# Sums of squares of x as four 32-row tiles, a bank copy and one product, in a two-group transformer trunk on one core

## The chip, the cores and the metric

The kernel runs on one core of a Trainium2 chip. The metric is device time in microseconds (us) of one execution; lower is better. TensorE (PE in the rows) multiplies, VectorE (DVE) and ScalarE (ACT) do elementwise work, GpSimd (POOL) splits weights, and SyncE (SP) issues the weight transfers.

## What is computed

Two layers are applied to 128 context tokens and 256 latent tokens at once (384 token columns, width 1024). Each layer has three sub-layers: a SwiGLU FFN, a token mixer (differential attention, a gated recurrence, grouped attention), and a second FFN. Each is wrapped in the same way:

```python
def rmsnorm(x, g):
    xf = x.astype(jnp.float32)
    xf = xf * lax.rsqrt(jnp.mean(xf * xf, axis=-1, keepdims=True) + EPS)
    return (xf * g.astype(jnp.float32)).astype(x.dtype)

def modulate(x, g, shift, scale):
    return rmsnorm(x, g) * (1 + scale) + shift

mod = jax.nn.silu(cond) @ p['ada_w'][l] + p['ada_b'][l]
m = jnp.split(mod[:, None, :], 9, axis=-1)
h = modulate(x, p['norm_pre'][l, 0], m[0], m[1])
y = swiglu(h, p['ffn_gate'][l, 0], p['ffn_up'][l, 0], p['ffn_down'][l, 0])
x = x + 0.5 * m[2] * rmsnorm(y, p['norm_post'][l, 0])
```

So ahead of each sub-layer there is one mean of squares of x per token (the subject here), behind it one mean of squares of y, and the nine modulation vectors of a layer come from a matrix `ada_w` of 1024 x 9216.

## The kernel before

Activations lie transposed: the 1024 channels are eight tiles of 128 partitions (`KT` is 8), the 384 tokens (`T`) are the free dimension. Weights come in units of 512 KB. For a weight unit ScalarE makes a rounded copy `w_hi` (`highs`), GpSimd the rest `w_lo` (`lows`), and TensorE takes three products for each block (line 573). A modulation unit (`ada_unit`, line 612) is 128 rows of `ada_w` by 1024 columns; TensorE multiplies it by the small `c_col` in four column tiles of 32, side by side, into a bank of `MOD`.

All orders are written out by hand, one program for each engine, and semaphores tie them. The order of the transfers on SyncE's queue is the list `ALL`. A transfer into one of the four `raw` places waits until the unit that held the place has been used (`lo_ready` for weights, `ada_used` for modulation units). Eighteen further modulation units are loaded early into places named `hold`, `hold_a` and so on.

Between two sub-layers lies a gap (`gap`), of which there are five. In it TensorE first sums the squares of y (`y_sums`), runs the first half of the gap's modulation units, sums the squares of x (`x_sums`), runs the second half of the units, and goes on with the next sub-layer's weights (`by_tiles`), which wait for the normalized rows `h` tile by tile. Four of the gaps have 24 units, so 12 and 12; the last one, ahead of the second FFN of layer 1, has 8, all of them in hold places. In the four long gaps units 14 to 17, 22 and 23 use the `raw` ring; unit 22 takes the place of unit 14 and unit 23 that of unit 15. Units 14 and 15 stand behind `x_sums`.

In a gap VectorE makes 1/root of y (line 1487), updates x (1490, 1492, 1495), scales x (1454), makes 1/root of x (1465) and normalizes (1459); ScalarE squares x (1072), takes the square roots (1050) and makes `h_hi` (1079), and VectorE `h_lo` (1445).

At the start (the prologue) the same sums run with modulation units 4, 5 and 6 of a first group of 16 between them: a unit behind every second product. Those 16 units wait for their transfers only. There `first_pre` on VectorE takes the root, multiplies x by it (1425), takes the first modulation group (1322, 1324), makes the scale factors mA in three small steps (1408 to 1410), multiplies by them (1432) and takes the second group.

Of the kernel before, what the change touches and what calls it, by code (L numbers as in the profile page):

```python
# [9 lines left out]
D, SEQ, LAT, DEPTH, PAST = 1024, 128, 256, 2, 128  # L10
T = SEQ + LAT
NB = T // 128
KT = D // 128
# [43 lines left out]
def build(nc, io, out):  # L57
    f32, f32r, u8 = mybir.dt.float32, mybir.dt.float32r, mybir.dt.uint8
    ALU, ACT, AX = mybir.AluOpType, mybir.ActivationFunctionType, mybir.AxisListType
# [6 lines left out]
    def at(name, shape, dt, offset):  # L66
        size = (int(np.prod(shape[1:])) * (1 if dt == u8 else 4) + 31) // 32 * 32
        return nc.alloc_sbuf_tensor_at(name, shape, dt, offset=offset), offset + size

    x, o = at("x", [128, KT, T], f32, base)  # L70

    hold, _ = at("hold", [128, 6, 1024], f32, o)
    h_hi, o = at("h_hi", [128, KT, T], f32r, o)
    h_lo, o = at("h_lo", [128, KT, T], f32r, o)
    raw, o = at("raw", [128, RAW, 1024], f32, o)
    w_hi, o = at("w_hi", [128, SPLIT, 1024], f32r, o)
    w_lo, o = at("w_lo", [128, SPLIT, 1024], f32r, o)
    R = o
    act_hi, o = at("act_hi", [128, FT, T], f32r, R)
    act_lo, R_END = at("act_lo", [128, FT, T], f32r, o)  # L80
    x_out, _ = at("x_out", [128, NB, D], f32, R)
# [9 lines left out]
    hold_b, _ = at("hold_b", [128, 3, 1024], f32, R + FT * T * 4)  # L91
    hold_a, _ = at("hold_a", [128, 4, 1024], f32, R + 4 * T * 4)
# [19 lines left out]
    y, o = at("y", [128, KT, T], f32, Y)  # L112
    sq, o = at("sq", [128, KT, T], f32, o)
    hold_sq, _ = at("hold_sq", [128, 3, 1024], f32, o - KT * T * 4)
    silu, o = at("silu", [128, 2, T], f32, o)
    prod, o = at("prod", [128, 2, T], f32, o)
    Y_END = Y + 36864
    assert o <= Y_END
    y_sum, o = at("y_sum", [128, T], f32, o)
    root, o = at("root", [128, T], f32, o)  # L120
    ada_t, o = at("ada_t", [128, 256], f32, o)
    assert o <= Y_END
    rows, o = at("rows", [128, 3, 128], f32, Y)
    x_rows, o = at("x_rows", [128, NB, D], f32, o)

    first_w, o = at("first_w", [128, 16, 1024], f32, R)
    lam_in, o = at("lam_in", [128, DEPTH, 4, 64], f32, o)
    lam_p, o = at("lam_p", [128, DEPTH * 2, 64], f32, o)
    mask_f, o = at("mask_f", [128, 2, len(LEVELS), 64], f32, o)
    assert o <= R_END  # L130

    ctx_k, o = at("ctx_k", [128, 512], f32, Y)
    ctx_v, o = at("ctx_v", [128, 512], f32, o)
    ctx_kT, o = at("ctx_kT", [128, HA, 128], f32, o)
    v_nat, o = at("v_nat", [128, NB, 512], f32, o)
    k_nat, o = at("k_nat", [128, 512], f32, o)
    p = []
    for b in range(2):
        t_, o = at(f"p{b}", [128, 2, T], f32, o)
        p.append(t_)  # L140
    pT, o = at("pT", [128, 2, T], f32, o)
    comb, o = at("comb", [128, T], f32, o)
    rope_t, o = at("rope_t", [128, 4, LAT], f32, o)
    rope_u, o = at("rope_u", [128, 4, LAT], f32, o)
    assert o <= Y_END
    ctx_ck, o = at("ctx_ck", [128, 128], f32, Y)
    ctx_cv, o = at("ctx_cv", [128, 128], f32, o)
    c_kT, o = at("c_kT", [128, PAST + T], f32, o)
    c_kd, o = at("c_kd", [128, KVC, PAST + T], f32, o)
    c_nat, o = at("c_nat", [128, 512], f32, o)  # L150
    c_vd, o = at("c_vd", [128, KVC, 4, 2, 64], f32, o)
    assert o <= Y + 14 * 1024
    c_sq, o = at("c_sq", [128, 5, T], f32, Y + 18432)
    c_rt, o = at("c_rt", [128, 5, T], f32, o)
# [5 lines left out]
    for b in range(2):  # L160
        t_, o = at(f"dec{b}", [128, 2 * T], f32, o)
        dec.append(t_)
    lev = []
    for b in range(2):
        t_, o = at(f"lev{b}", [128, 2 * T], f32, o)
        lev.append(t_)
    W1 = o
    scores, o = at("scores", [128, HB * T], f32, o)
    v_b, o = at("v_b", [128, NB, HB, 128], f32, o)
    b_f, o = at("b_f", [128, HB * T], f32, o)  # L170
    b_b, o = at("b_b", [128, HB * T], f32, o)
    assert o == Y_END
    k_sum, _ = at("k_sum", [128, HB * T], f32, W1)
    scan_b, _ = at("scan_b", [128, HB * T], f32, S_IN)
    q_st, o = at("q_st", [128, 2, HB, LAT], f32, W0)
    k_st, o = at("k_st", [128, HB, 256], f32, o)
    assert o == W1
    o_sq, o = at("o_sq", [128, HB, T], f32, W0)
    o_rt, o = at("o_rt", [128, HB, T], f32, o)
# [7 lines left out]
    o = Y_END  # L187
    con, o = at("con", [128, C_N], f32, o)
    masks, o = at("masks", [128, 2, len(LEVELS), 64], u8, o)
    o = (o + 31) // 32 * 32  # L190
    reset, o = at("reset", [128, T], f32, o)
    vec, o = at("vec", [128, DEPTH, V_ROWS], f32, o)
    misc, o = at("misc", [128, M_ROWS], f32, o)
    mod, o = at("mod", [128, MOD_TILES, 2], f32, o)
    tick, o = at("tick", [128, 1], f32, o)
    tick_a, o = at("tick_a", [128, 1], f32, o)
    c_col, o = at("c_col", [128, KT, 32], f32, o)
    mA, o = at("mA", [128, KT, 2], f32, o)
    mB, o = at("mB", [128, KT, 2], f32, o)
    mG, o = at("mG", [128, KT, 2], f32, o)  # L200
    eps, o = at("eps", [128, 1], f32, o)
    lam_s, o = at("lam_s", [128, DEPTH, 2], f32, o)
    neg_lam, o = at("neg_lam", [128, DEPTH], f32, o)
    lb, o = at("lb", [128, DEPTH, 2, HB], f32, o)
    omlb, o = at("omlb", [128, DEPTH, 2, HB], f32, o)
    lb_d, o = at("lb_d", [128, 2, HB], f32, o)
    sub_g, o = at("sub_g", [128, DEPTH], f32, o)
    qn_g, o = at("qn_g", [128, DEPTH], f32, o)
    one_l, o = at("one_l", [128, 8], f32, o)
    lbl, o = at("lbl", [128, 2, 2, HB], f32, o)  # L210
    nmax, o = at("nmax", [128, 2, 2], f32, o)
    esum, o = at("esum", [128, 2, 2], f32, o)
    rsum, o = at("rsum", [128, 2], f32, o)
    ends, o = at("ends", [128, 2, HB * NB], f32, o)
    dend, o = at("dend", [128, 2, HB], f32, o)
    assert o <= nc.sbuf_usable_end, (o, nc.sbuf_usable_end)

    ident, ones = con[:, C_ID:C_ID + 128], con[:, C_ONE:C_ONE + 128]
    head_ones, swap = con[:, C_HEAD:C_HEAD + 128], con[:, C_SWAP:C_SWAP + 128]

    with ExitStack() as ctx:
        def pb(name, shape):
            return ctx.enter_context(nc.psum_tensor(name, shape, f32))

        X = [pb("X0", [128, 2, 512]), pb("X1", [128, 2, 512])]
        Ab = pb("Ab", [128, 512])
        S5, S6, S7 = pb("S5", [128, 512]), pb("S6", [128, 512]), pb("S7", [128, 512])
# [5 lines left out]
        def sem(name):  # L233
            return ctx.enter_context(nc.semaphore(name))
# [7 lines left out]
        x_free = [sem("x0_free"), sem("x1_free")]  # L242
        g_free = [sem(f"g{b}_free") for b in range(4)]
        names = ("const_in table_in mask_in rows_in lam_in_s lam_ready x_in xs_in rows_turned vec_ready c_ready c_zero x_turned x_copied x_ready "
                 "x_sq_ready y_sq_ready y_added sum_ready root_ready norm_ready hh_ready h_ready silu_ready act_ready "
                 "dve_step act_step half_done gate_ready gate_free sum_made mg_hi_ready ada_used ada_copied mod_taken "
                 "proj_ready ctx_in nat_ready nat_copied nat_out swap_ready rope_done scores_ready max_ready "
                 "probs_ready comb_ready turned_ready turned_copied out_ready out_taken "
# [5 lines left out]
        S = {n: sem(n) for n in names}  # L254
# [302 lines left out]
        def _(pe):  # L557
            seen = Seen()
# [126 lines left out]
            def x_sums(units):  # L685

                for k in range(KT):
                    pe.wait_ge(S["x_sq_ready"], seen.next("x_sq_ready"))
                    mm = nc.tensor.matmul(S5[:, 0:T], ones, sq[:, k, :], start=k == 0, stop=k == KT - 1)  # L689
                    if k % 2 and k // 2 < len(units):  # L690
                        ada_unit(units[k // 2])
                mm.then_inc(S["sum_ready"], 1)

            def head_sums():

# [239 lines left out]
            for b in range(NB):  # L935
# [5 lines left out]
                for k in range(KT):  # L941
                    bank = (S7, S5)[k // 4][:, :] if b == 2 else X[b][:, k // 4, :]
                    mm = nc.tensor.transpose(bank[:, k % 4 * 128:k % 4 * 128 + 128],
                                             x_rows[:, b, k * 128:k * 128 + 128], ident)
# [23 lines left out]
            for c in range(4):  # L968
                pe.wait_ge(S["x_ready"], KT + 3 * KT * DEPTH - KT + 2 * c + 2)
                for b in range(NB):  # L970
                    for k in (2 * c, 2 * c + 1):
                        mm = nc.tensor.transpose(banks[b][k // 4][:, k % 4 * 128:k % 4 * 128 + 128],
                                                 x[:, k, b * 128:b * 128 + 128], ident)
# [5 lines left out]
        def _(act):  # L979
            seen = Seen()  # L980
            A = nc.scalar.activation
# [65 lines left out]
            def root_of_sums():  # L1047

                act.wait_ge(S["sum_ready"], seen.next("sum_ready"))
                A(root[:, :], S5[:, 0:T], ACT.Sqrt, bias=eps[:, 0:1], scale=1.0 / D).then_inc(S["root_ready"], 1)  # L1050

            def gap(units):

                root_of_sums()

                act.wait_ge(S["ada_used"], units[2].n + 1)
                x_squares(0, KT)
                root_of_sums()
                act.wait_ge(S["ada_used"], units[:9][-1].n + 1)
                h_highs(0, KT)  # L1060

# [196 lines left out]
            A(omlb[:, 1, :, :], lb_d[:, :, :], ACT.Sigmoid, scale=-1.0)  # L1258
            A(tick_a[:, :], eps[:, :], ACT.Sqrt)
            x_squares(0, KT)  # L1260
            root_of_sums()
            highs(2)
            h_highs(0, 2)
            highs(SPLIT)
# [685 lines left out]
```

## Time and profile before

| | us |
|---|---|
| median of 3 runs | 2328.82 (2327.84 to 2329.07) |
| profiled execution, its own time | 2327.03 |
| its span, first to last instruction | 2325.2 |
| PE busy | 2207.0 (95%) |
| DVE busy | 961.5 (41%) |
| ACT busy | 889.8 (38%) |
| POOL busy | 1274.0 (55%) |
| mean granted TensorE clock | 0.976 |

The rows give a start, a duration, an engine, a line and the tiles that are written and read; in brackets stands how long the engine was idle before and what it waited for. An fp32 product of one matmul in the source is two instructions in the rows (x2).

### The profile page before, as it was taken

The numbers are of one execution on the slowest core, as the hardware profiler recorded it, in microseconds if no ns is written. First come the engines' busy times: TensorE is split into PE (matmuls) and PEld (weight loads), VectorE is DVE, ScalarE is ACT, GpSimd is POOL, SyncE is SP. The second block draws the span as 40 slices with busy tenths as digits, with TensorE's granted clock in tenths as the row PEclk, the third lists the DMA queues.
The fourth block names the chain that finished last, engine by engine and source line by source line (L and its number), as shares of the span: only waits on it lengthen the run. The fifth ranks groups of instructions, "written<-read, shape, count | busy, mean of one in ns | idle before, by whom it ended". The sixth has DMA issues, their size and how long they took to land.

```text
span 2325.2 us, 32769 instructions
## 1 busy us (share of the span) xinstructions
PE 2207.0 (95%) x13545; PEld 2083.2 (90%) x13545; DVE 961.5 (41%) x1532; ACT 889.8 (38%) x1181; POOL 1274.0 (55%) x988
## 2 busy tenths in 40 slices
PE   6999999998999999999999999999798999899998
PEld 4999988987899897999979999799688989799997
DVE  5221125535778365212251221634376874622112
ACT  3222223345644444233233233324474535332331
POOL 2666554433498463666646666354346954466662
PEclk8999999999999999999999999999899999899998
DMA  7555774322222274444554445633222234344431
GB/s 272 163 162 168 247 238 141 97 83 75 73 64 74 91 279 138 127 127 163 192 189 127 127 150 195 209 118 92 68 73 64 73 96 151 98 118 126 128 117 65
DMA packets 306924, 311.42 MB, mean 134 GB/s; under 512 B 9923, under 2 KB 285655, under 8 KB 306775
## 3 DMA queue, kind: packets, MB, share of 16 engines
q1 hardware_dynamic: 299671, 303.55, 41.2%
q10 hardware_dynamic: 7104, 5.77, 0.8%
q8 instruction: 107, 1.75, 0.3%
q14 instruction: 42, 0.34, 0.0%
HBM read 305.35 MB, written 3.93 MB: 133 GB/s over the span
## 4 chain that ended last, share of the span: by engine, by line
PE 77%; DVE 11%; ACT 7%; issue 2%; DMA 2%; POOL 1%; SPq 0%; ACTq 0%; DVEq 0%
PE X L573 54%; PE S L573 8%; PE Ab L573 5%; PE X L814 2%; DMA raw<-in_ada_w 1%; PE S L689 1%; ACT w_hi L990 1%; PE X L732 1%; PE S L761 1%; ACT p L1126 1%; DVE mg_lo L1376 1%; DVE y L1490 1%; PE X L712 1%; DVE x L1492 1%; DVE root L1487 1%
## 5 line engine op out<-in xcount | busy, mean ns | idle before, releaser
L514 POOL TENSOR_TENSOR w_lo<-raw,w_hi 128x512 fp32r<-128x512 f32 (+1 forms) x872 | 1168.0, 1361 | 995.8 <-ACT w_hi L990 986.0
L990 ACT ACTIVATE w_hi<-raw 128x1024 fp32r<-128x1024 f32 (+1 forms) x436 | 453.3, 1041 | 729.7 <-PE X L573 688.1
L573 PE MATMUL X<-h_hi,w_hi 128*128 128x384 f32 x1600 | 539.9, 337 | 9.1 <-DVE h_lo L1445 9.1
L573 PE MATMUL X<-h_hi,w_lo 128*128 128x384 f32 x1600 | 537.4, 336 | 0.0
L573 PE MATMUL X<-h_lo,w_hi 128*128 128x384 f32 x1600 | 537.4, 336 | 0.0
L573 PEld LDWEIGHTS X<-h_hi,w_hi 128*128 128x128 f32 x1600 | 302.5, 189 | 18.2 <-DVE h_lo L1445 10.8
L573 PEld LDWEIGHTS X<-h_lo,w_hi 128*128 128x128 f32 x1600 | 302.6, 189 | 0.0
L573 PEld LDWEIGHTS X<-h_hi,w_lo 128*128 128x128 f32 x1600 | 302.4, 189 | 0.0
L1501 DVE TENSOR_TENSOR prod<-X,silu 128x768 f32<-128x768 f32 x44 | 42.1, 958 | 571.1 <-PE X L573 571.1
L573 PE MATMUL X<-act_hi,w_hi 128*128 128x384 f32 x704 | 236.2, 335 | 0.0
L573 PE MATMUL X<-act_hi,w_lo 128*128 128x384 f32 x704 | 235.3, 334 | 0.0
L573 PE MATMUL X<-act_lo,w_hi 128*128 128x384 f32 x704 | 235.2, 334 | 0.0
L1512 DVE TENSOR_SCALAR y<-X,mG 128x128 f32<-128x128 f32 x96 | 33.4, 412 | 339.4 <-ACT prod L1094 339.4
L573 PE MATMUL S<-h_hi,w_hi 128*128 128x384 f32 x480 | 167.9, 350 | 0.0
L573 PE MATMUL S<-h_lo,w_hi 128*128 128x384 f32 x480 | 161.8, 337 | 0.0
L573 PE MATMUL S<-h_hi,w_lo 128*128 128x384 f32 x480 | 161.5, 337 | 0.0
L573 PEld LDWEIGHTS X<-act_hi,w_hi 128*128 128x128 f32 x704 | 132.1, 188 | 3.7 <-issue 3.7
L573 PEld LDWEIGHTS X<-act_lo,w_hi 128*128 128x128 f32 x704 | 132.1, 188 | 0.0
L573 PEld LDWEIGHTS X<-act_hi,w_lo 128*128 128x128 f32 x704 | 132.1, 188 | 0.0
L573 PE MATMUL Ab<-h_hi,w_hi 128*128 128x384 f32 x320 | 111.8, 349 | 0.7 <-DVE acc_e L1363 0.7
L573 PE MATMUL Ab<-h_hi,w_lo 128*128 128x384 f32 x320 | 107.9, 337 | 0.0
L573 PE MATMUL Ab<-h_lo,w_hi 128*128 128x384 f32 x320 | 107.9, 337 | 0.0
(339 smaller groups left out, 3242.8 us busy)
## 6 DMA issues: line engine op xcount, KB each, us to landing
raw<-in_w_in SPq DMA_DIRECT2D x124, 512.0 KB, 3.8
raw<-in_ffn_gate SPq DMA_DIRECT2D x88, 512.0 KB, 3.8
raw<-in_ffn_up SPq DMA_DIRECT2D x88, 512.0 KB, 3.7
raw<-in_ffn_down SPq DMA_DIRECT2D x80, 512.0 KB, 3.4
raw<-in_ada_w SPq DMA_DIRECT2D x48, 512.0 KB, 4.2
hold<-in_ada_w SPq DMA_DIRECT2D x29, 512.0 KB, 4.6
first_w<-in_ada_w SPq DMA_DIRECT2D x16, 512.0 KB, 10.5
hold_a<-in_ada_w SPq DMA_DIRECT2D x16, 512.0 KB, 6.8
```

The lines of the kernel that those rows point to most:

```text
L514: ins = nc.gpsimd.tensor_tensor(slot(w_lo, u)[:, part], raw_of(u)[:, part], slot(w_hi, u)[:, part], SUB)
L573: mm = nc.tensor.matmul(dst, w[:, k, m * 128:m * 128 + 128], r_, start=start and k + j == 0, stop=stop and k == u.nk - 1 and j == 2)
L689: mm = nc.tensor.matmul(S5[:, 0:T], ones, sq[:, k, :], start=k == 0, stop=k == KT - 1)
L712: mm = nc.tensor.matmul(X[xb][:, t // 2, t % 2 * 256:t % 2 * 256 + 256], swap, proj[:, tile0 + t, SEQ:T], start=True, stop=True)
L732: mm = nc.tensor.matmul(X[n % 2][:, c, at_:at_ + k.shape[-1]], proj[64 * c:64 * c + 64, (AQ if kind == "a" else CQ) + h, b * 128:b * 128 + ...
L761: mm = nc.tensor.matmul((S5, S6)[c][:, 0:128], v, pT[:, c, j * 128:j * 128 + 128], start=j == 0, stop=j == len(kbs) - 1)
L814: mm = nc.tensor.matmul(X[n % 2][:, 0, j * 64:j * 64 + 64], g, cols, start=True, stop=True)
L990: A(slot(w_hi, u), raw_of(u), ACT.Copy).then_inc(hi_ready[u.split], 1)
L1126: e = A(p[n % 2][:, c, 0:w], X[n % 2][:, c, 0:w], ACT.Exp, bias=nmax[:, n % 2, c:c + 1], accum_out=esum[:, n % 2, c:c + 1])
L1376: V.tensor_tensor(mg[t][1][:, t % 4, :], gate_b[:, t, :], mg[t][0][:, t % 4, :], SUB).then_inc(S["mg_ready"], 1)
L1501: V.tensor_tensor(prod[:, :, :], X[1][:, :, 0:T], silu[:, :, :], MUL).then_inc(x_free[1], 1)
L1512: ins = V.tensor_scalar(y[:, 2 * i + m, t0:t1], X[u.dest][:, m, t0:t1], mG[:, 2 * i + m, g:g + 1], None, MUL)
```

## The change

The eight products of `x_sums` (one for each tile k of squares) no longer add up in one full bank. Product k uses 32 columns of ones and writes 32 rows of the bank S5, at column tile k % 4; tiles k and k + 4 add up in the same 32 rows. ScalarE copies the bank to a new tile `part`, and one fp32 product with the full matrix of ones adds the 128 rows, each part being there 32 times, which the factor 1/(32 D) takes out again. It writes X[0]. ScalarE's root waits for that. TensorE's wait for the copy and the added product stand ahead of the modulation units that follow `x_sums`.

```diff
+    part, _ = at("part", [128, T], f32, o - T * 4)
...
             def x_sums(units):
...
                 for k in range(KT):
+                    rows_ = slice(32 * (k % 4), 32 * (k % 4) + 32)
                     pe.wait_ge(S["x_sq_ready"], seen.next("x_sq_ready"))
-                    mm = nc.tensor.matmul(S5[:, 0:T], ones, sq[:, k, :], start=k == 0, stop=k == KT - 1)
+                    mm = nc.tensor.matmul(S5[rows_, 0:T], ones[:, 0:32], sq[:, k, :], start=k < 4, stop=k >= 4,
+                                          tile_position=(0, 32 * (k % 4)))
                     if k % 2 and k // 2 < len(units):
                         ada_unit(units[k // 2])
-                mm.then_inc(S["sum_ready"], 1)
+                mm.then_inc(S["part_ready"], 1)
+
+                pe.wait_ge(S["part_copied"], seen.next("part_copied"))
+                nc.tensor.matmul(X[0][:, 0, 0:T], ones, part[:, :], start=True, stop=True).then_inc(S["sum_ready"], 1)
...
+            def root_of_parts():
+
+                act.wait_ge(S["part_ready"], seen.next("part_ready"))
+                A(part[:, :], S5[:, 0:T], ACT.Copy).then_inc(S["part_copied"], 1)
+                act.wait_ge(S["sum_ready"], seen.next("sum_ready"))
+                A(root[:, :], X[0][:, 0, 0:T], ACT.Sqrt, bias=eps[:, 0:1], scale=1.0 / (32 * D)).then_inc(S["root_ready"], 1)
...
                 x_squares(0, KT)
-                root_of_sums()
+                root_of_parts()
```

`root_of_parts` takes the place of `root_of_sums` in `gap` (behind the squares of x, not behind those of y) and in the prologue.

On TensorE in a long gap, from the first 12 modulation units on (hold places) to the second 12, before the change:

```order
L612 MATMUL S<-hold_sq,c_col 32x256 x12
L612 MATMUL S<-hold,c_col 32x256 x20
L612 MATMUL Ab<-hold,c_col 32x256 x4
L612 MATMUL Ab<-hold_c,c_col 32x256 x8
L612 MATMUL Ab<-hold_b,c_col 32x256 x4
L689 MATMUL S<-sq,con 128x384 x8
L612 MATMUL Ab<-hold_b,c_col 32x256 x8
L612 MATMUL Ab<-raw,c_col 32x256 x8
L612 MATMUL S<-raw,c_col 32x256 x8
L612 MATMUL S<-hold_a,c_col 32x256 x16
```

The same place in the changed kernel (`con` holds the ones):

```order
L614 MATMUL S<-hold,c_col 32x256 x20
L614 MATMUL Ab<-hold,c_col 32x256 x4
L614 MATMUL Ab<-hold_c,c_col 32x256 x8
L614 MATMUL Ab<-hold_b,c_col 32x256 x4
L693 MATMUL S<-sq,con 32x384 x8
L700 MATMUL X<-part,con 128x384
L614 MATMUL Ab<-hold_b,c_col 32x256 x8
L614 MATMUL Ab<-raw,c_col 32x256 x8
L614 MATMUL S<-raw,c_col 32x256 x8
L614 MATMUL S<-hold_a,c_col 32x256 x16
```

The product of line 700 now stands between the sums and unit 12; two units later come 14 and 15 (Ab<-raw), whose use lets units 22 and 23 be transferred.

On TensorE in the prologue, before the change:

```order
L612 MATMUL Ab<-first_w,c_col 32x256 x16
L689 MATMUL S<-sq,con 128x384 x2
L612 MATMUL Ab<-first_w,c_col 32x256 x4
L689 MATMUL S<-sq,con 128x384 x2
L612 MATMUL Ab<-first_w,c_col 32x256 x4
L689 MATMUL S<-sq,con 128x384 x2
L612 MATMUL Ab<-first_w,c_col 32x256 x4
L689 MATMUL S<-sq,con 128x384 x2
L612 MATMUL Ab<-first_w,c_col 32x256 x4
L612 MATMUL S<-first_w,c_col 32x256 x32
```

The same place in the changed kernel:

```order
L614 MATMUL Ab<-first_w,c_col 32x256 x16
L693 MATMUL S<-sq,con 32x384 x2
L614 MATMUL Ab<-first_w,c_col 32x256 x4
L693 MATMUL S<-sq,con 32x384 x2
L614 MATMUL Ab<-first_w,c_col 32x256 x4
L693 MATMUL S<-sq,con 32x384 x2
L614 MATMUL Ab<-first_w,c_col 32x256 x4
L693 MATMUL S<-sq,con 32x384 x2
L700 MATMUL X<-part,con 128x384
L614 MATMUL Ab<-first_w,c_col 32x256 x4
L614 MATMUL S<-first_w,c_col 32x256 x32
```

Products and units keep their order; products are 32 rows high, and line 700 stands behind the last of them.

## Rows read from the trace of the kernel before

**Rows 1.** The page, the chain that ended last, shares by engine.

```profile
PE 77%; DVE 11%; ACT 7%; issue 2%; DMA 2%; POOL 1%; SPq 0%; ACTq 0%; DVEq 0%
```

**Rows 2.** Chain through the first long gap (355 us): start, duration, what.

```profile
355.32 1.91 PE Ab L612 x32
357.23 0.02 issue
357.25 5.23 DMA raw<-in_ada_w
...
362.52 0.64 PE S L612 x8
363.16 11.99 PE X L573 x68
```

**Rows 3.** Timeline of the same gap, ScalarE, VectorE and TensorE.

```profile
353.19 0.99 ACT L1072 ACTIVATE sq<-x 128x384 f32<-128x384 f32 x2 [0.53 <-DVE x L1495]
355.36 0.58 ACT L1050 ACTIVATE root<-S,eps 128x384 f32<-128x384 f32 x1 [1.18 <-PE S L689]
360.12 0.75 DVE L1445 SCALAR_TENSOR_TENSOR h_lo<-sq,mB,h_hi 128x128 fp32r<-128x128 f32 x2
361.17 0.64 PE L612 MATMUL S<-raw,c_col 128*32 128x256 f32 x8 [1.39 <-DMA raw<-in_ada_w]
```

**Rows 4.** Timeline ahead of that gap: one lone fp32 product behind ScalarE.

```profile
340.08 0.81 ACT L1094 ACTIVATE prod<-X 128x768 f32<-128x768 f32 x1 [0.96 <-PE X L573]
340.94 0.91 PE L682 MATMUL S<-prod,con 128*128 128x384 f32 x2 [0.26 <-ACT prod L1094]
```

**Rows 5.** Groups of ScalarE by form: copies out of a bank (busy, mean ns).

```profile
L1027 ACT ACTIVATE gates<-S 128x384 f32<-128x384 f32 x22 | 10.7, 486 | 20.2 <-PE S L573 20.2
```

**Rows 6.** Waits in the second, third and fourth long gap: us in total, times, longest.

```profile
PE S L612 <- DMA raw<-in_ada_w: 2.5, 2, 1.6
...
PE S L612 <- DMA raw<-in_ada_w: 1.6, 2, 1.0
...
PE S L612 <- DMA raw<-in_ada_w: 1.3, 2, 0.7
```

**Rows 7.** Timeline of the short gap (2015 us).

```profile
2015.01 8.26 PE L689 MATMUL S<-sq,con 128*128 128x384 f32 x16 [4.13 <-ACT sq L1072]
...
2019.70 0.99 ACT L1072 ACTIVATE sq<-x 128x384 f32<-128x384 f32 x2 [0.53 <-DVE x L1495]
2023.30 0.58 ACT L1050 ACTIVATE root<-S,eps 128x384 f32<-128x384 f32 x1 [2.61 <-PE S L689]
2028.86 0.69 PE L573 MATMUL X<-h_hi,w_hi 128*128 128x384 f32 x1 [3.73 <-DVE h_lo L1445]
```

**Rows 8.** Stretches: busy by engine, then granted clock, DMA share, GB/s.

```profile
17.00:21.00 4.00, 4.00 (x25) 1.59 (x24) 0.00 (x0) 1.77 (x5) 0.00 (x0) 1.00 1.03 410
41.00:47.70 6.70, 5.69 (x18) 5.69 (x19) 4.70 (x9) 6.70 (x17) 2.47 (x2) 0.50 0.18 56
1194.70:1198.10 3.40, 3.40 (x12) 3.40 (x12) 3.40 (x12) 1.83 (x6) 0.00 (x0) 0.50 1.07 344
2014.00:2020.60 6.60, 5.59 (x9) 3.17 (x10) 6.32 (x10) 3.71 (x8) 0.00 (x0) 0.50 0.02 6
```

**Rows 9.** Timeline of the prologue.

```profile
15.36 3.41 ACT L1072 ACTIVATE sq<-x 128x384 f32<-128x384 f32 x8 [4.76 <-DVE x L1820]
15.60 0.64 PE L612 MATMUL Ab<-first_w,c_col 128*32 128x256 f32 x8 [0.17 <-DMA first_w<-in_ada_w]
...
23.93 0.58 ACT L1050 ACTIVATE root<-S,eps 128x384 f32<-128x384 f32 x1 [5.16 <-PE S L689]
30.09 5.41 POOL L514 TENSOR_TENSOR w_lo<-raw,w_hi 128x512 fp32r<-128x512 f32 x4 [29.65 <-ACT w_hi L990]
34.34 1.19 DVE L1410 TENSOR_TENSOR mA<-mA,vec 128x16 f32<-128x16 f32 x1
35.57 3.76 DVE L1432 TENSOR_SCALAR sq<-sq,mA 128x128 f32<-128x128 f32 x16
40.03 0.18 DVE L1403 TENSOR_TENSOR mB<-mod,vec 128x16 f32<-128x16 f32 x1
42.01 0.69 PE L573 MATMUL X<-h_hi,w_hi 128*128 128x384 f32 x1 [5.33 <-DVE h_lo L1445]
```

More of the change, by code:

```diff
@@ L244, in build @@
         names = ("const_in table_in mask_in rows_in lam_in_s lam_ready x_in xs_in rows_turned vec_ready c_ready c_zero x_turned x_copied x_ready "
-                 "x_sq_ready y_sq_ready y_added sum_ready root_ready norm_ready hh_ready h_ready silu_ready act_ready "
+                 "x_sq_ready y_sq_ready y_added sum_ready part_ready part_copied root_ready norm_ready hh_ready h_ready silu_ready act_ready "
                  "dve_step act_step half_done gate_ready gate_free sum_made mg_hi_ready ada_used ada_copied mod_taken "
@@ L1260, in _ @@
             x_squares(0, KT)
-            root_of_sums()
+            root_of_parts()
             highs(2)
```

## The prediction

> **What bounds the kernel now.** I read the chain that ended last first. TensorE holds 77% of it [rows 1], so work that only VectorE or ScalarE does counts where TensorE stands still for it. The sums of x stand in six places: the prologue, four long gaps and one short gap. For each the question is which wait of TensorE ends last behind the sums, so I followed the chain through each place, and then the timeline.
>
> In the first long gap the chain runs from the sums' end at 355.32 through the modulation units behind them, and at 357.25 it leaves TensorE for a transfer of a modulation unit (5.23 us), returns for the last unit at 362.52 and goes on with the weights at 363.16 [rows 2]. The transfer is that of unit 23 into the raw place of unit 15. It can't be issued before unit 15 has been used, and unit 15 stands behind the sums. So the start of the next sub-layer hangs on the *end of the sums on TensorE*, not on the root. The rows of h are early: the first h_lo is made by 360.87, 2.3 us ahead of the weights' start [rows 3]. In the other three long gaps TensorE waits for the same two transfers, 2.5, 1.6 and 1.3 us [rows 6].
>
> In the short gap all units are in hold places. There TensorE waits 3.73 us for h_lo [rows 7], so the root decides. In the prologue TensorE waits 5.33 us for h_lo too [rows 9], and the root decides through VectorE's long row of steps.
>
> **The change part by part, long gap.** Before: ScalarE's last square of x ends at 354.18 (353.19 + 0.99), and the root starts at 355.36, 1.18 us later [rows 3]. After:
>
> - The last square's product. In the full array it had to queue behind that of k = 6; in its own 32 columns it can start at once, at 354.23 (a product starts 0.05 after the ScalarE instruction that releases it: 340.89 to 340.94 [rows 4]). How long does a lone product last in a 32-column tile? A modulation unit is such a product with 256 columns, four side by side: 0.64 us for all four [rows 9]. The two passes of 384 columns take 2 x 128 columns more; a lone full product of 384 columns takes 0.91 [rows 4]. Between 0.64 and 0.91 I take 0.64 and the added columns at 2 x 0.107, less what the rows round, 0.84: end at 355.07. That is 0.25 earlier than now (355.32).
> - The copy. Out of a bank, 128x384, 0.486 us [rows 5], from 355.11 (the root starts 0.04 behind the sums' end now, 355.32 to 355.36) to 355.59.
> - The product. 0.05 and 0.91 [rows 4]: 355.64 to 356.56. The root starts at 356.60.
>
> So the root and everything that TensorE does behind the sums come 356.60 - 355.36 = **1.24 us later**. No table is loaded for the copy: ScalarE already makes copies (w_hi) between roots and squares. Nothing else is queued on ScalarE between squares and root; on TensorE the 12 units are queued behind the wait, and SyncE's queue waits for two of them, with the transfers of the next weights behind. Units 14 and 15, the two issues, the transfers, the last unit and the weights' start all move by 1.24. The rows of h move by the same and keep their 2.3 us. Behind the gap TensorE is the bound again, so nothing gives the time back. Four long gaps: **+4.96**. Bounds for one gap: +1.49 if the tiles don't run side by side (nothing saved ahead of the copy), and about 0 if the last transfers didn't depend on the sums.
>
> Where would the work that the tiles save show? Eight full products take 0.64 each in a row, 5.1 us, four tiles side by side about 1.3. The Trainium skill (TensorEngine Tiling (Array Packing), section Theoretical Speedup) gives up to four times for such tiles; by it alone a gap would lose 3.9 us. The trace disagrees for the gaps: TensorE waits for squares, which wait for x, and only the last 1.14 us (354.18 to 355.32) lie behind the last square.
>
> **Short gap.** The clock is at half (0.50, the 1.2 GHz level) from 2014.0 to 2020.6 [rows 8], after TensorE stood idle for 4.13 us. At that level the full products fall behind the squares: the last square ends at 2020.69, the root starts at 2023.30, 2.61 later [rows 7]. With tiles side by side the first six products keep up (two squares come every 1.9 us, two tiles take 1.3 to 1.5 at half clock), the last ends at about 2021.6, and copy and product bring the root to 2023.15: **-0.1**. If the clock is still at half then, both products take longer and the root comes at 2024.6: +1.3.
>
> **Prologue.** The squares are all there at 18.77 (15.36 + 3.41), TensorE finishes the sums at 23.9 [rows 9]: here TensorE is behind. A pair of products side by side takes 0.64 plus a tail, a unit 0.43; the sums are then held by unit 6, which stands ahead of the last pair. Unit 3 was waited for at 15.60 [rows 9]; at 410 GB/s [rows 8] 0.524 MB need 1.28 us, so unit 6 lands at 19.44. The last pair ends at 19.9 + 0.83 = 20.7, the copy at 21.3, the product at 22.2; the root starts at 22.26 instead of 23.93, 1.67 earlier.
>
> Not all of it arrives. GpSimd makes w_lo from 30.09 to 35.5 [rows 9], and while it does, VectorE's steps take as long as GpSimd's: 1.19 us for 128x16 at 34.34, against 0.18 for such a step at 40.03. The two take turns. Now the copy to mod and the three mA steps lie in that time, and the 16 multiplications follow alone at 35.57 in 3.76. Moved 1.67 ahead, VectorE gets through the copy and two steps before 30.09; the third step and about three multiplications then take a turn each, and the other 13 (3.76 x 13/16 = 3.0) begin at 35.1 to 35.5. They end at 38.1 to 38.5 instead of 39.3, 0.8 to 1.2 earlier; I take 1.0. TensorE starts its weights at 41.0 instead of 42.01. There the clock is at half until 47.7 [rows 8]; 1.0 us at half is worth 0.5 at full clock: **-0.5**. Bounds: 0, and -2.3, if the clock also comes back one stretch of 3.4 us (as that at 1194.7 [rows 8]) earlier, because TensorE is busy sooner (-1.7 more).
>
> **Sum.** 4 x 1.24 - 0.1 - 0.5 = +4.4. The profiled execution took 2327.03, 1.8 under the median of the runs; on its own time that gives 2331.4, on the median of 2328.82 **2333.2 us**. A measurement of this kernel tells 0.2% (4.7 us) from no change, so the forecast lies just inside that.
>
> **The rivals.**
>
> - *The clock falls more often.* TensorE uses a quarter or half of its columns in the sums and stands still for another 0.6 us per gap. One more stretch of 3.4 us at half costs up to 1.7 us where TensorE is the bound. For: the short gap and the stretch at 1194.7 [rows 8] show that such idle times cost clock; against: modulation units in 32-column tiles leave it at full in the other long gaps. Two or three stretches more: +7.8 to +9.5, 2336.6 to 2338.3.
> - *The tiles don't run side by side.* Gaps +1.49 x 4, short gap +1.3, prologue about +0.3: +7.6, 2336.4. Against it, four tiles of a unit fit in 0.64 us [rows 9].
> - *The delay is hidden in the long gaps*, because the transfers have their own reason to end late, or h's slack takes it: -0.6 to +0.6, 2328 to 2329.5. Against it is the chain of rows 2.
> - *Faster: TensorE is what is behind in the gaps.* This decides as soon as the squares wait ready for TensorE; the tiles must save more than the 1.49 of copy and product, and now 1.14 in all lie behind the last square in a long gap. With all eight squares ready a gap's sums would take 1.3 + 0.2 + 1.49 = 3.0 instead of 5.3, -2.3 in five gaps, with the prologue -12, 2317. The skill's page on tiling would have it so. For it speaks only the short gap at half clock.
>
> **How the numbers follow.** As forecast, one stretch of clock more or less included (+2.7 to +6.1, 2331.5 to 2335): 0.58, of it 0.31 under +4.7 and 0.27 over. Clock 0.15, tiles in series 0.06, hidden 0.16, faster by the tiles or by several stretches of clock 0.05. Faster by over 0.2%: 0.05; within: 0.31 + 0.16 = 0.47; slower: 0.27 + 0.15 + 0.06 = 0.48. The range runs from 2329.0 (the upper part of hidden, or -2.3 in the prologue with a stretch less) to 2338.0 (two stretches more).
>
> **What would show it.** Root of x 2.4 us behind the last square instead of 1.18 in the long gaps; units 22 and 23 issued and the weights started 1.24 later, seen from the root of y; in the short gap the root 2.5 behind the last square; in the prologue the root near 22.3, but TensorE's first weights only near 41. Wrong would be: weights that start no later in the long gaps (the transfers were not tied to unit 15), sums' products that follow each other at 0.64 in a tile column, or a granted clock with other half stretches than now.

## The result, and the profile after

| | before | after |
|---|---|---|
| median of 12 runs each | 2328.45 us | 2333.57 us |
| lowest to highest | 2324.96 to 2331.08 | 2330.14 to 2336.73 |
| ratio, 95% interval | 1 | 1.0023 (1.0016 to 1.0031) |
| span of the profiled execution | 2325.2 us | 2333.7 us |
| granted clock over the span | 0.976 | 0.975 |

The changed kernel is 5.1 us slower by the medians, just over the 0.2% (4.7 us) that can be told from no change. The two profiled spans differ by more, 8.5 us. All tables below say which of the two they use.

**Where TensorE is held.** The page of the kernel after, the chain that ended last, shares by engine. It answers to [rows 1] and has hardly moved; a change of 5 us in 2330 can't be seen there.

```profile
PE 77%; DVE 11%; ACT 7%; issue 2%; DMA 1%; POOL 1%; SPq 0%; ACTq 0%; DVEq 0%
```

**The first long gap.** First ScalarE's timeline of the kernel after, which answers to the ScalarE rows of [rows 3]: start, duration, operation, and in brackets the idle time ahead and what ended it.

```profile
351.81 0.99 ACT L1087 ACTIVATE sq<-x 128x384 f32<-128x384 f32 x2 [0.52 <-DVE x L1510]
353.73 0.49 ACT L1063 ACTIVATE part<-S 128x384 f32<-128x384 f32 x1 [0.92 <-PE S L693]
355.22 0.58 ACT L1065 ACTIVATE root<-X,eps 128x384 f32<-128x384 f32 x1 [1.00 <-PE X L700]
```

The last square ends at 352.80 and the root starts at 355.22, 2.42 us later; before it was 1.18 [rows 3]. Between them now stand two waits of ScalarE, 0.92 and 1.00, with the copy in the middle. TensorE's timeline of the same gap:

```profile
352.39 1.30 PE L693 MATMUL S<-sq,con 128*32 128x384 f32 x4 [0.21 <-ACT sq L1087]
354.27 0.91 PE L700 MATMUL X<-part,con 128*128 128x384 f32 x2 [0.58 <-ACT part L1063]
355.12 1.07 PE L614 MATMUL Ab<-hold_b,c_col 128*32 128x256 f32 x16
...
360.83 0.64 PE L614 MATMUL S<-raw,c_col 128*32 128x256 f32 x8 [1.19 <-DMA raw<-in_ada_w]
362.12 0.64 PE L614 MATMUL S<-raw,c_col 128*32 128x256 f32 x8 [0.65 <-DMA raw<-in_ada_w]
362.69 0.45 PE L575 MATMUL X<-h_hi,w_hi 128*128 128x384 f32 x1
```

The sums end at 353.69, 0.89 behind the last square (before 1.14): that is all that the tiles give here. Then TensorE waits 0.58 for the copy, and the product takes 0.91. Only at 355.12 do the twelve modulation units begin. The chain through the gap, as in [rows 2]:

```profile
353.73 0.50 ACT part L1063
354.23 0.04 issue
354.27 0.91 PE X L700 x2
355.19 1.91 PE Ab L614 x32
357.10 0.02 issue
357.11 4.96 DMA raw<-in_ada_w
...
362.12 0.64 PE S L614 x8
362.76 12.36 PE X L575 x70
```

It is the chain of [rows 2] with two links put in front, the copy and the product: then four units, the transfer of unit 23, the last unit, the weights. One row of VectorE's timeline, which answers to the h_lo row of [rows 3], shows that the rows of h still don't decide; they are there at 360.73, 2.0 us ahead of the weights:

```profile
359.98 0.75 DVE L1460 SCALAR_TENSOR_TENSOR h_lo<-sq,mB,h_hi 128x128 fp32r<-128x128 f32 x2
```

TensorE's waits for transfers in the second, third and fourth long gap (us in total, times, longest) answer to [rows 6]:

```profile
PE S L614 <- DMA raw<-in_ada_w: 3.4, 2, 1.9
...
PE S L614 <- DMA raw<-in_ada_w: 1.8, 2, 1.0
...
PE S L614 <- DMA raw<-in_ada_w: 1.2, 2, 0.6
```

In the third and fourth the waits are about as long as before (1.6 and 1.3): everything, issue and landing, has moved by the same amount. In the second they are 0.9 longer.

**The short gap.** Timelines of TensorE and ScalarE of the kernel after, as in [rows 7]:

```profile
2023.31 6.76 PE L693 MATMUL S<-sq,con 128*32 128x384 f32 x16 [4.13 <-ACT sq L1087]
2030.65 0.91 PE L700 MATMUL X<-part,con 128*128 128x384 f32 x2 [0.58 <-ACT part L1063]
2028.01 0.99 ACT L1087 ACTIVATE sq<-x 128x384 f32<-128x384 f32 x2 [0.53 <-DVE x L1510]
2031.61 0.58 ACT L1065 ACTIVATE root<-X,eps 128x384 f32<-128x384 f32 x1 [1.00 <-PE X L700]
```

The root starts 2.61 behind the last square (2029.00 to 2031.61), as before. The sums take 6.76 instead of 8.26, and copy and product take it all back. Over the traces it varies a little: 2.42 to 2.63 in the five that have tiles there, 2.60 to 2.83 in the four with full sums and no added steps.

**The prologue.** Timelines of TensorE, ScalarE, VectorE and GpSimd, as in [rows 9]. The multiplications (L1447) stand three times: all of them, those that begin before 35.0, and those from there on, each from a view of its own:

```profile
16.67 0.86 PE L693 MATMUL S<-sq,con 128*32 128x384 f32 x4
20.18 0.82 PE L693 MATMUL S<-sq,con 128*32 128x384 f32 x4
21.59 0.91 PE L700 MATMUL X<-part,con 128*128 128x384 f32 x2 [0.59 <-ACT part L1063]
22.54 0.58 ACT L1065 ACTIVATE root<-X,eps 128x384 f32<-128x384 f32 x1 [1.00 <-PE X L700]
30.20 0.17 DVE L1424 TENSOR_SCALAR mA<-mA 128x16 f32<-128x16 f32 x1
30.29 4.99 POOL L516 TENSOR_TENSOR w_lo<-raw,w_hi 128x512 fp32r<-128x512 f32 x4 [29.84 <-ACT w_hi L998]
30.41 1.17 DVE L1425 TENSOR_TENSOR mA<-mA,vec 128x16 f32<-128x16 f32 x1
31.61 6.76 DVE L1447 TENSOR_SCALAR sq<-sq,mA 128x128 f32<-128x128 f32 x16
31.61 3.74 DVE L1447 TENSOR_SCALAR sq<-sq,mA 128x128 f32<-128x128 f32 x3
35.28 3.09 DVE L1447 TENSOR_SCALAR sq<-sq,mA 128x256 f32<-128x256 f32 x13
41.05 0.69 PE L575 MATMUL X<-h_hi,w_hi 128*128 128x384 f32 x1 [4.13 <-DVE h_lo L1460]
```

The root starts at 22.54 instead of 23.93, the weights at 41.05 instead of 42.01. GpSimd's four steps end at 35.28. Of the 16 multiplications three stand beside them and take 3.67 us from start to start (1.22 each, as long as a step of GpSimd); the other 13 follow in 3.09 (0.24 each).

**Each stage.** Both traces, us. "Root to root" is from the start of the root of y to that of x. The prologue's row has the two absolute times.

| | root to root, before | after | root of y to weights, before | after | moved |
|---|---|---|---|---|---|
| prologue (times of root and weights) | 23.93 | 22.54 | 42.01 | 41.05 | -0.96 |
| long gap 1 | 12.82 | 14.06 | 20.55 | 21.53 | +0.98 |
| long gap 2 | 12.82 | 14.06 | 20.95 | 23.52 | +2.57 |
| long gap 3 | 12.82 | 14.06 | 20.07 | 21.49 | +1.42 |
| long gap 4 | 13.17 | 14.41 | 20.13 | 21.28 | +1.15 |
| short gap | 14.25 | 14.25 | 19.81 | 19.81 | 0.00 |

The last column sums to +5.2; I call it the *stage sum*. The rest of the 8.5 us between the spans, 3.4 us, lies between the stages, from the weights' start to the next root of y, where the clock stands otherwise. Windows of the kernel after: the stretch, busy by engine, then granted clock, DMA share, GB/s.

```profile
40.00:46.30 6.30, 5.25 (x16) 5.25 (x17) 4.26 (x9) 6.30 (x16) 2.02 (x2) 0.50 0.37 119
899.60:906.50 6.90, 6.21 (x24) 5.40 (x25) 6.62 (x20) 4.66 (x11) 0.00 (x0) 0.51 0.73 251
```

The first is the stretch at half that [rows 8] has at 41.0 to 47.7: it now ends at 46.3. The second is not in the trace before. It begins in the second long gap, behind 1.50 and 1.89 us in which TensorE waited for the last two transfers. The change is not needed for it: the kernel of the first experiment, whose gaps are those of before, is at half from 898.2 to 901.6, behind waits of 1.63 and 1.86. Leaving out the stretches at the very end of the program, the trace before has 95.6 us at half and that after 105.8; with them it is 112.0 and 118.5.

### The profile page after: what moved, and what is told of

Read it like the earlier page. It is cut to its first block, busy times and chain, and to the rows that moved or that the text cites. A ratio compares the mean times of both kernels' runs of the same rounds, so it can differ in the third digit from the quotient of the medians.

```text
span 2333.7 us, 32799 instructions
## 1 busy us (share of the span) xinstructions
PE 2207.2 (95%) x13557; PEld 2077.8 (89%) x13557; DVE 960.2 (41%) x1532; ACT 892.7 (38%) x1187; POOL 1273.0 (55%) x988
## 4 chain that ended last, share of the span: by engine, by line
PE 77%; DVE 11%; ACT 7%; issue 2%; DMA 1%; POOL 1%; SPq 0%; ACTq 0%; DVEq 0%
PE X L575 54%; PE S L575 8%; PE Ab L575 4%; PE X L822 2%; DMA raw<-in_ada_w 1%; ACT w_hi L998 1%; PE X L740 1%; DVE y L1505 1%; PE S L769 1%; ACT p L1141 1%; PE Ab L614 1%; DVE mg_lo L1391 1%; DVE root L1502 1%; DVE x L1507 1%; PE X L720 1%
```

## The experiments

All are kernels of their own, with the kernel before run beside them on the same chip. Three changes of code are used in them: the *sums* (full array or tiles), the *split* of a long gap's units (12 ahead of the sums and 12 behind, or 16 and 8), and what stands between sums and root (nothing, or copy and product).

### The prologue alone

The tiles, copy and product stay in the prologue; the gaps have the full sums of the kernel before again (`x_sums_full`).

```diff
                 for u in units[:len(units) // 2]:
                     ada_unit(u)
-                x_sums([])
+                x_sums_full([])
...
                 x_squares(0, KT)
-                root_of_parts()
+                root_of_sums()
```

> Tiled sums with copy and product in the prologue only; the five gaps sum as before. Theory (each long gap pays the copy and the product, the prologue gains): the root of the prologue near 22.4 instead of 23.93, the weights start near 41.0, every gap 12.8 us from the root of y to the root of x as before, and the time 0.5 to 1.4 us under before: 2327.0 to 2328.0. Rival (the clock, not the gaps, made the changed kernel slower): the time lies between before and the changed kernel by chance, with no difference in the gaps. Rival (GpSimd's turns swallow the prologue's gain): weights start at 42.0, time as before.

Measured: 2327.46 against 2327.32, ratio 0.9998 (0.9989 to 1.0006). Root at 22.53, weights at 40.94, the gaps' roots where they are before (12.82 in the first three, 1.18 behind the last square). The prologue gives about a microsecond at the weights' start, and the time of the whole kernel, of which I had expected 0.5 to 1.4 less, can't tell that from nothing.

### The gaps alone

```diff
-            x_sums(PHASES["first"][4:7])
+            x_sums_full(PHASES["first"][4:7])
...
             x_squares(0, KT)
-            root_of_parts()
+            root_of_sums()
```

> Tiled sums in the five gaps only; the prologue sums as before. Theory: from the root of y to the root of x 14.06 us in the long gaps (1.24 more than 12.82), about 14.2 in the short one, and the time 4 x 1.24 = 5.0 us over before and about 1 over the changed kernel: 2333.5 to 2334.5. Rival (the clock made the difference): nearer to before than +2.5.

Measured: 2336.2, ratio 1.0037 (1.0024 to 1.005). All four long gaps have the root 2.42 behind the last square and root to root 14.05 (14.40 in the fourth), +1.23 or +1.24 each. The loss is in the gaps. It is larger than expected by about 2 us: 3.1 us more were lost to the clock in its executions than in those of the kernel before (below), and its prologue was late by 0.9 (weights at 42.92).

### Full sums, but copy and product kept

It tells the price of the two added steps from the gain of the tiles. (The sum over all 128 partitions is taken twice here, so the scale is 1/(128 D).)

```diff
-                    mm = nc.tensor.matmul(S5[rows_, 0:T], ones[:, 0:32], sq[:, k, :], start=k < 4, stop=k >= 4,
-                                          tile_position=(0, 32 * (k % 4)))
+                    mm = nc.tensor.matmul(S5[:, 0:T], ones, sq[:, k, :], start=k == 0, stop=k == KT - 1)
```

> The sums are full products in the whole bank as before, but the copy and the added product stay (scale 1/(128 D)), in all six places. Theory: the tiles save 0.25 in a long gap, so without them a long gap takes 12.82 + 1.49 = 14.3 us from root to root, the short gap 1.5 to 1.8 more than with tiles or before (15.8), and the prologue's root comes at 25.4 instead of 22.5; in all 4 x 1.49 + 1.5 + 0.2 to 0.5 = +7.7 to +8.0 over before: 2336.3. Rival (the tiles save nothing, or cost, because TensorE changes its tile mode): long gaps at 14.06 as in the changed kernel or under it.

Measured: 2337.79, ratio 1.0041 (1.0026 to 1.0056), 10.5 over before where I had expected 7.7 to 8.0. The weights start 9.9 later in sum: 6.5 in the long gaps, 1.7 in the short one and 1.7 in the prologue, for which I had put 0.2 to 0.5. TensorE's timeline of its first long gap:

```profile
353.16 3.02 PE L693 MATMUL S<-sq,con 128*128 128x384 f32 x8 [0.37 <-ACT sq L1086]
356.76 0.91 PE L699 MATMUL X<-part,con 128*128 128x384 f32 x2 [0.58 <-ACT part L1062]
```

The root comes 2.67 behind the last square: copy and product with their latencies cost 2.67 - 1.18 = 1.49 in a long gap, and the tiles save 2.67 - 2.42 = 0.25 of it. In the short gap, where TensorE is behind at half clock, the tiles save 4.29 - 2.61 = 1.68, and the steps cost the same (before, without either, it is 2.61 too); in the prologue the tiles save 25.53 - 22.54 = 3.0, and the steps cost about 1.2 (25.53 less 24.37, the mean of the root in the three traces that have full sums and no added steps there: 23.93, 24.79 and 24.38).

### All eight products in one tile column

As after, but the products use rows 0 to 31 of the bank, one behind the other, as one sum of eight (`start=k == 0, stop=k == KT - 1`); the copy has 32 rows and the product contracts over 32.

```diff
-                    rows_ = slice(32 * (k % 4), 32 * (k % 4) + 32)
+                    rows_ = slice(0, 32)
...
-                                          tile_position=(0, 32 * (k % 4)))
+                                          tile_position=(0, 0))
```

> The changed kernel with all eight products in the same 32 columns and rows, one behind the other; the copy takes 32 rows, the product 32 rows of part. Theory (what the tiles save is that products of different column tiles run side by side): in a long gap the last product waits for the one before, so the root of x comes 0.25 later than in the changed kernel, 14.3 us behind the root of y, and in the prologue each pair takes 1.3 us instead of 0.8, so that the root comes near 24.5 to 25.4 instead of 22.5. Rival (it is the 32 columns that are faster, not the four places): both as in the changed kernel.

Measured with a single execution: 2338.71, against 2328.68; the root comes 2.57 behind the last square in the long gaps, and in the prologue at 24.29. TensorE's timeline of its prologue:

```profile
20.57 0.49 PE L693 MATMUL S<-sq,con 128*32 128x384 f32 x1
20.89 0.59 PE L614 MATMUL Ab<-first_w,c_col 128*32 128x256 f32 x2
21.32 1.45 PE L693 MATMUL S<-sq,con 128*32 128x384 f32 x4
23.35 0.91 PE L700 MATMUL X<-part,con 32*128 32x384 f32 x2 [0.57 <-ACT part L1063]
```

Two products in one column take 1.45, in two columns 0.82. So the tiles of the change do run side by side. And a product over 32 partitions takes as long as one over 128 (0.91): a smaller partial doesn't make the added step cheaper.

### The product behind four units

If the wait of TensorE for the copy holds up the units, four of them can stand in front of it.

```diff
                 mm.then_inc(S["part_ready"], 1)
+                for u in behind:
+                    ada_unit(u)
```

with the first four units of the second half as `behind` in the long gaps.

> As the changed kernel, but in the four long gaps TensorE runs units 12 to 15 between the tiled sums and the wait for the copy. Theory (what passes the delay on is the transfer that waits for unit 15, and h has 2.3 us of slack): root of x some 0.3 later than in the changed kernel (14.4 from root to root), but units 14 and 15 used 0.25 earlier than before, so the weights start as before or 0.2 earlier, and the time is before less the prologue's gain: 2327 to 2328. Rival (the root and h decide, the transfer only happens to end with them): no better than the changed kernel, 2333.5 to 2335.

Measured: 2331.23, ratio 1.0015 (1.0005 to 1.0025), over 3 us slower than I expected. TensorE's timeline of its first long gap shows what I had overlooked:

```profile
353.34 0.49 PE L695 MATMUL S<-sq,con 128*32 128x384 f32 x1
353.41 0.85 PE L614 MATMUL Ab<-hold_b,c_col 128*32 128x256 f32 x9
...
355.48 0.91 PE L704 MATMUL X<-part,con 128*128 128x384 f32 x2
356.33 1.07 PE L614 MATMUL S<-raw,c_col 128*32 128x256 f32 x16
...
361.99 0.44 PE L575 MATMUL X<-h_hi,w_hi 128*128 128x384 f32 x1 [1.15 <-DVE h_lo L1464]
```

The product waits for nothing now, but it stands behind four units of 0.43 and starts at 355.48 instead of 354.27 + 0.13 (the copy starts 0.13 later in this trace). The root comes 3.49 behind the last square, 1.07 later than in the kernel after; I had written 0.3. That eats h's slack, and the weights wait 1.15 for h_lo. They start 20.68 behind the root of y, 0.13 behind the gap of before, and about 0.8 ahead of after; in the other three long gaps they start 0.27 earlier, 0.62 and 0.93 later than before. The wait has changed its owner, from transfer to h, at nearly the same place. The stage sum is +0.2, yet the medians differ by 3.9; its executions lost 2.9 us more to the clock, and about 1 us I can't place.

### Sixteen units ahead of the sums

The chain of the gap says that the transfer of unit 23 waits for unit 15. Moving four units to the front frees that place before the sums, in the kernel before and in that after.

```diff
-                for u in units[:len(units) // 2]:
+                half = 16 if len(units) == GAP else len(units) // 2
+                for u in units[:half]:
                     ada_unit(u)
                 x_sums([])
-                for u in units[len(units) // 2:]:
+                for u in units[half:]:
                     ada_unit(u)
```

Before with this edit:

> The kernel before with one edit: in the four long gaps 16 modulation units stand ahead of the sums of x and 8 behind, so that units 14 and 15 are used, and the transfers of 22 and 23 issued, some 7 us sooner. Theory (the transfer that waits for unit 15 ends last in a long gap): TensorE no longer waits for those transfers; the weights start when the first h_lo is there, 18.5 to 18.7 us behind the root of y instead of 20.1 to 20.9, so 4 x 1.5 to 2.3 = 6 to 9 us less, 2318 to 2322. Rival (root and h decide, or TensorE's own work): the weights start no earlier, time as before.

After with it:

> The changed kernel with the same edit (16 units ahead of the tiled sums, copy and product). Theory: the root now decides through h, and the copy and product stand in it, so against e4_units_ahead each long gap is about 1.2 us longer from the root of y to the weights (19.7 to 19.9), in all 4 x 1.2 - 0.5 to 1.4 = +3.4 to +4.3 over e4_units_ahead, but 4 x 1.0 to 1.8 under the changed kernel: 2322 to 2326. Rival (the cost came through the transfers alone): as fast as e4_units_ahead or faster.

Measured: 2323.33 (ratio 0.9977, 0.9968 to 0.9985) and 2323.85 (0.9979, 0.997 to 0.9988), against 2328.68. The first gained 5.4 us where I had expected 6 to 9. TensorE's timeline of the first long gap, in the kernel before with the edit:

```profile
348.08 1.04 PE L612 MATMUL Ab<-raw,c_col 128*32 128x256 f32 x16
349.06 5.84 PE L690 MATMUL S<-sq,con 128*128 128x384 f32 x16
...
360.49 0.44 PE L573 MATMUL X<-h_hi,w_hi 128*128 128x384 f32 x1 [2.00 <-DVE h_lo L1446]
```

and in the kernel after with it:

```profile
352.35 1.30 PE L694 MATMUL S<-sq,con 128*32 128x384 f32 x4 [0.21 <-ACT sq L1088]
354.24 0.91 PE L701 MATMUL X<-part,con 128*128 128x384 f32 x2 [0.58 <-ACT part L1064]
...
360.74 0.45 PE L575 MATMUL X<-h_hi,w_hi 128*128 128x384 f32 x1 [2.00 <-DVE h_lo L1461]
```

In both, the units end early, no transfer is waited for, and TensorE waits 2.00 for h_lo. The root decides. The weights start 18.37 and 19.61 behind the root of y: the same 1.24 as without the edit, now through h. So the delay does not depend on who waits. The medians don't show it: +0.5 between the two where the stage sums say +2.9 and I had expected +3.4 to +4.3. The kernel with full sums lost 3.5 us more to the clock than the one with tiles; with that taken out as below, the two differ by 3.1.

### Tiles in the prologue, full sums and 16 units ahead in the gaps

The edits of the first and of the last experiment together.

```diff
+                half = 16 if len(units) == GAP else len(units) // 2
...
-                x_sums([])
+                x_sums_full([])
```

> Tiled sums, copy and product in the prologue only (as e1_prologue_only), and 16 units ahead of the full sums in the long gaps (as e4_units_ahead). Theory: both gains add up, e4_units_ahead less 0.5 to 1.4: 2317 to 2321, the fastest of all. Rival: the prologue's gain is given back and it equals e4_units_ahead.

Measured: 2321.0, ratio 0.9974 (0.9963 to 0.9984), the fastest of all. Weights at 41.03 in the prologue and 18.37 to 18.74 behind the root of y in the long gaps.

### The kernel after once more

Unedited, to see how far the clock share accounts for its time.

> The changed kernel once more, unedited, beside before on one chip, with the granted clock of every execution of both. The stages account for +5.1 us in the profiled executions (weights start 6.1 later in sum in the long gaps, short gap 0, prologue -1.0); the clock's share is (1 - mean clock) x time. Theory (stages and clock are all there is): the difference of the medians is 5.1 plus the difference of the clock's shares, within 1.5; with equal clocks +5. Theory 2 (most of it is the clock): the clock's shares differ by 3 or more, and what is left is 2 or less.

Measured: 2334.82 against 2329.27, ratio 1.0027 (1.0016 to 1.0038): +5.6, again close to the first comparison's +5.1. The share of the clock was as large as the one theory asked (3.2 us more than before), but the sum of both terms was too high by 2.7; the other theory's bound for the rest (at most 2) was passed too: 5.6 - 3.2 = 2.4 by the medians, 3.1 by the means. Neither holds as written. A slope of 1 for the clock is too much; with the one below the rest is +4.1.

### The account

Every execution comes with a span and a granted clock; (1 - clock) x span is the time that it lost to the clock at most. Over 139 executions a kernel's own times follow this number, with 0.67 us of time for 1 us of it (correlation 0.79). "Rest" is the difference of the mean times less 0.67 x the difference in clock, its interval from the 1.39 us by which a single execution still scatters then. The stage sum is worked out as in the table above, from one trace each.

| against before | medians | means | lost to clock | rest (95%) | stage sum |
|---|---|---|---|---|---|
| prologue alone | +0.1 | -0.5 | +1.5 | -1.5 ± 1.0 | +0.3 |
| gaps alone | +8.9 | +8.6 | +3.1 | +6.5 ± 1.2 | +7.0 |
| full sums, copy and product | +10.5 | +10.1 | 0.0 | +10.1 ± 1.2 | +9.9 |
| product behind four units | +3.9 | +3.3 | +2.9 | +1.3 ± 1.0 | +0.2 |
| 16 units ahead, full | -5.4 | -5.7 | +2.3 | -7.2 ± 1.0 | -7.1 |
| 16 units ahead, tiled | -4.8 | -4.9 | -1.2 | -4.1 ± 1.0 | -4.2 |
| best of both | -7.7 | -6.7 | +3.1 | -8.8 ± 1.2 | -8.6 |
| after once more | +5.6 | +6.3 | +3.2 | +4.1 ± 1.0 | +5.4 |

Rest and stage sum agree within 1.3 us but for the first row (1.8), where one trace has a second long gap with a late transfer (22.12 instead of 20.95). The one-column kernel, with a single execution, is left out; its stage sum is +9.0.

## Why the prediction was right

The forecast of 2333.2 was 0.4 from the median, by steps that mostly came out as written, and by errors of two terms that partly cancel. Part of the closeness is luck: the forecast was +4.4 on a median of 2328.82, and beside the changed kernel before had 2328.45, so the difference is +5.1.

- **Last product in its own tile column.** Forecast 0.84 from its start and 0.25 won; measured 0.25, and the kernel with full sums and both steps gives the same 0.25. Had the tiles run in series, the root would have come 0.15 later (2.57 behind the square in the one-column kernel), not 0.25: even there the products keep up with the squares.
- **Copy, product, root.** Forecast 0.486, 0.91 and 1.24 in all; measured 0.49, 0.91, and +1.24 in each of the four long gaps to the hundredth.
- **Passed on to the weights.** Forecast +1.24 per gap through unit 15 and unit 23's transfer, +4.96. Measured +0.98, +2.57, +1.42, +1.15, together +6.1. The way is that of the forecast, and moving unit 15 ahead of the sums shows it: the waits for transfers vanish. The size of one trace is off, mainly in the second gap, where unit 23 landed 5.61 us behind the end of its issue (5.26 before) and the clock fell behind the waits. But this excess of 1.2 us wanders. In the second trace of the same kernel the first gap has +3.33 and the second +0.63, and the unchanged gaps of the prologue-alone kernel come out at -0.20, +1.17, +0.34 and +0.03, together +1.3. So the traces don't tell +6.1 from +4.96.
- **Short gap.** Forecast -0.1, measured 0.0. The last pair ends 1.07 behind the last square, not 0.9.
- **Prologue.** Root forecast 22.26, came at 22.54; the last pair ended at 21.00 instead of 20.7. It was held by unit 6, as forecast: this landed at 19.67 instead of 19.44, and TensorE began it at 19.71. Weights forecast 41.0, came at 41.05. The turns with GpSimd came as written too: the copy and two steps stood ahead of them (0.17 to 0.18 each), the third step (1.17) and three multiplications in them, and the other 13 began at 35.28, in the forecast 35.1 to 35.5; they ended at 38.37, in the forecast 38.1 to 38.5. The Trainium skill (SBUF — State Buffer, Who interferes with whom) describes the port pair that VectorE and GpSimd share as an exclusive lock, held for a whole instruction. The trace is in line with that: 1.22 us against 0.24 for one multiplication. The *value* of this term was mis-sized: forecast -0.5, because the clock would stay at half until 47.7. The stretch at half ended at 46.3, the microsecond was kept whole, and the next root of y starts 1.38 earlier. Over all traces the weights start at 40.84 to 41.05 with tiles in the prologue (six traces) and at 42.01 to 42.92 with full sums and no added steps (three, of which that of before is the earliest): 1.5 us on the mean, and the next root of y comes 1.45 earlier on the mean. So the gain is kept; why is not shown. The end of the stretch lies between 44.8 and 46.3 with tiles and between 46.2 and 47.8 with full sums, but it doesn't follow the weights one by one (weights at 42.92 and end at 46.9 in one trace, 42.01 and 47.8 in another).
- **Sum.** +6.1 - 1.0 = +5.2 (unrounded +6.12 - 0.96) in the stage table, against +5.0 - 0.6 = +4.4 of the forecast. One slip lies in the range: its upper end, 2338.0, is called two stretches more, which by the forecast's own sum is 2336.6; three give 2338.3.

**The rivals.** *Hidden in the long gaps* falls by the stage table. *Tiles in series* falls by the one-column kernel. *TensorE is behind, so it gets faster* holds in the prologue and, at half clock, in the short gap, and nowhere else; in a long gap the tiles have 0.25 to save against 1.49. The Trainium skill (TensorEngine Tiling (Array Packing), Theoretical Speedup) promises up to four times for such tiles; two of them do run in 0.82 us instead of 1.45, but a product that waits for its input has nothing of it. *The clock falls more often* was partly so: the trace after has 6.5 us more at half in all, and on the mean of the second comparison 3.2 us more were lost, worth about 2 us. As written, with 2336.6 to 2338.3, it did not come. Nor do the runs tie it to the tiles or the added steps: the kernels without them in the gaps lost 1.5, 2.3 and 3.1 us more than before, and that with full sums, copy and product nothing more.

**What stays open.** Why the changed kernel and some variants lose more to the clock than others, and so how much of the 5.1 us is the change itself: the rest in the second comparison is +4.1 ± 1.0. Some of the added stretches stand behind waits of TensorE ahead of the weights, as at 899.6, but the kernel with 16 units ahead and full sums has a 2.00 us wait there in every long gap and lost 3.5 us more than its tiled twin, which has the same wait. No run here separates that.

## What to carry to other kernels

Ask of a reduction in TensorE not how long its products take but how much of them lies behind the last input. Here it was 1.14 of 5 us, so packing four tiles could save 0.25, while every step added between the last input and its reader (copy 0.49, product 0.91, two releases) is paid in full; the same edit pays where inputs are waiting, as in the prologue.

When a wait for a transfer ends a gap, look for the instruction that frees its buffer and move that ahead of the serial part. Four units moved to the other side of the sums gave 5.4 us, a little more than the whole change cost, and that they would give something could be read from the chain.

## What the runs showed of the hardware

- An fp32 product of 384 columns takes 0.91 us alone whether it contracts over 128 partitions or 32.
- Beside GpSimd's steps of the prologue (1.22 us from start to start) VectorE's take as long as these: a multiplication 1.22 us instead of 0.24, a step on 128x16 1.17 instead of 0.18.
- Two products of 32 output rows in different tile columns overlap fully (0.82 for both), in the same column they don't (1.45). In a long gap the one-column kernel (root 2.57 behind the last square) lies nearer to full sums with both steps (2.67) than to the tiles (2.42).
- Times of one kernel scatter by 0.1 to 0.2% with the time its clock stands at half, 0.67 us for each microsecond of (1 - clock) x span. Two versions can differ by 1.24 us in each of four gaps in their traces and by 0.5 us in their medians.
